# Last three MoE blocks added from on-chip rows by one-hot products, the picked rows read back earlier, overflow rows accumulated into the outputs

## What is computed

```python
def hierarchical_moe(h, w_rg, b_rg, w_re, b_re, w_gate, w_up, w_down):
    ...                       # top-1 of 4 groups, top-2 of the 8 experts in it, gate (tokens x 32)
    for g in range(N_EXPERT_GROUPS):
        sl = slice(g * EXPERTS_PER_GROUP, (g + 1) * EXPERTS_PER_GROUP)
        hid = jax.nn.silu(jnp.einsum('td,edf->tef', t, w_gate[sl])) * jnp.einsum('td,edf->tef', t, w_up[sl])
        hid = hid * gate[:, sl, None].astype(hid.dtype)
        out = out + jnp.einsum('tef,efd->td', hid, w_down[sl])

xp = xp + mp[5] * hierarchical_moe(modulate(xp, norm_ffn_g[l], mp[3], mp[4]), ...)   # gate2 * moe
xs = xs + ms[5] * hierarchical_moe(modulate(xs, norm_ffn_g[l], ms[3], ms[4]), ...)
```

## Time and profile before

| | us |
|---|---|
| median of 3 runs | 822.14 (821.49 to 822.38) |
| the profiled execution, own time | 822.25 |
| its span | 820.5 |
| PE busy | 741.6 (90%) |
| DVE busy | 419.3 (51%) |
| ACT busy | 205.7 (25%) |
| POOL busy | 168.1 (20%) |
| the 16 DMA engines, mean over the span | 224 GB/s |

### The profile page before, as it was taken

The page is one execution under the profiler, slowest core; times in us unless marked ns, Lnnn a source line. Parts: engine busy times, 40 slices in busy tenths (PEclk is TensorE's granted clock), DMA queues, the critical chain, the costliest instruction groups (busy, mean ns, idle before and its releaser), DMA issues.

```text
span 820.5 us, 11125 instructions
## 1 busy us (share of the span) xinstructions
PE 741.6 (90%) x4203; PEld 456.2 (56%) x4203; DVE 419.3 (51%) x928; ACT 205.7 (25%) x417; POOL 168.1 (20%) x192
## 2 busy tenths in 40 slices
PE   4999988999999997999999999886999999999760
PEld 2344455578865655787888344544555555554320
DVE  4123399998799989300224524874333333332226
ACT  4013233314366775102000212222111111111100
POOL 2030012050000000253400002544223323322110
PEclk9899999999999999999999999987999999999995
DMA  8952032442056443343132913077999999999928
GB/s 344 406 174 88 1 102 72 150 171 84 24 205 222 189 169 139 113 142 131 60 103 77 367 75 124 28 261 302 425 424 421 426 423 426 424 424 428 397 98 312
DMA packets 25902, 183.63 MB, mean 224 GB/s; under 512 B 6460, under 2 KB 6884, under 8 KB 14456
## 3 DMA queue, kind: packets, MB, share of 16 engines
q1 hardware_dynamic: 15800, 161.06, 49.0%
q0 software_dynamic: 9456, 19.72, 7.2%
q10 hardware_dynamic: 592, 2.13, 0.7%
HBM read 178.59 MB, written 14.12 MB: 235 GB/s over the span
## 4 chain that ended last, share of the span: by engine, by line
PE 75%; DVE 9%; DMA 7%; ACT 4%; issue 2%; SPq 2%; POOL 0%; DVEq 0%; POOLq 0%; ACTq 0%
PE psum L735 22%; PE psum L1216 12%; PE psum L704 11%; PE psum L1230 6%; DMA arena<-in_experts 5%; PE psum L668 3%; PE psum L1117 2%; PE psum L614 2%; PE psum L1209 2%; ACT arena L1578 2%; DVE arena L2581 1%; DVE arena L2069 1%; PE psum L597 1%; DVE arena L2067 1%; DVE arena L2068 1%
## 5 line engine op out<-in xcount | busy, mean ns | idle before, releaser
L735 PE MATMUL psum<-hT,ring 128*128 128x260 f32 x640 | 143.1, 384 | 3.6 <-DVE sstat L2153 3.6
L735 PEld LDWEIGHTS psum<-hT,ring 128*128 128x128 f32 x640 | 120.7, 190 | 25.5 <-issue 6.3
L1578 ACT ACTIVATE arena<-psum 128x512 f32<-128x512 f32 (+10 forms) x130 | 69.4, 563 | 232.7 <-PE psum L735 74.0
L704 PE MATMUL psum<-ring,hT 128*128 128x512 f32 (+1 forms) x256 | 94.0, 520 | 0.0
L1216 PE MATMUL psum<-ring,arena 128*64 128x256 f32 x608 | 71.5, 389 | 3.2 <-DMA ring<-in_experts 3.2
L704 PEld LDWEIGHTS psum<-ring,hT 128*128 128x128 f32 x256 | 47.6, 191 | 44.9 <-issue 36.0
L1230 PE MATMUL psum<-arena 128*64 128x512 f32 x280 | 67.8, 605 | 3.3 <-issue 2.0
L1517 POOL DMA_INDIRECT expert_rows<-arena,router x35 | 35.3, 1008 | 156.3 <-DVE arena L2541 156.3
L1216 PEld LDWEIGHTS psum<-ring,arena 128*64 128x64 f32 x608 | 44.2, 140 | 34.1 <-issue 9.7
L2540 DVE SCALAR_TENSOR_TENSOR arena<-psum,router,arena 128x512 f32<-128x512 f32 x35 | 26.3, 751 | 64.6 <-PE psum L1230 64.6
L735 PE MATMUL psum<-arena,ring 128*128 128x260 f32 x256 | 58.6, 391 | 0.0
(11 more groups left out here) (380 smaller groups left out, 952.2 us busy)
## 6 DMA issues: line engine op xcount, KB each, us to landing
ring<-in_stream SPq DMA_DIRECT2D x21, 2048.0 KB, 7.9
ring<-in_experts SPq DMA_DIRECT2D x16, 2048.0 KB
arena<-in_experts SPq DMA_DIRECT2D x32, 1024.0 KB
arena<-in_experts SPq DMA_DIRECT2D x11, 2048.0 KB
hT<-in_experts SPq DMA_DIRECT2D x5, 2048.0 KB
ring<-expert_rows SPq DMA_DIRECT2D x8, 512.0 KB, 6.9
ring<-in_stream SPq DMA_DIRECT2D x2, 1280.0 KB, 5.6
arena<-in_x_prompt SPq DMA_DIRECT2D x4, 512.0 KB, 5.8
```

Source lines behind the costliest of these rows:

```text
L704: mm = pe.matmul(psum[:, b, 0:width], hT[:, k, t * P:(t + 1) * P], w[:, k, :], start=(k == 0), stop=(k == KD - 1))
L735: mm = pe.matmul(psum[:, b0 + s, 0:HALF], w[:, k, f * P:(f + 1) * P], rhs[:, k, s * HALF:(s + 1) * HALF], start=(first and k == 0), stop=( ...
L1578: ins = act.activation(out, in_, func, scale=scale)
```

## The change

1. Blocks 32, 33 and 34 (`N_LAST` = 3) are no longer scattered. Their scaled rows stay in three buffers (`y_of`: both `y_rows` and the free down buffer of pipeline place 29). For each of them DVE builds, at steps 6, 7 and 8, five one-hot matrices (`last_hots`: 128 x 128 for each prompt tile, 128 x 8 for the samples) that say which of the 128 half rows belongs to which token. After its last down product PE multiplies them with the kept rows (`last_products`): for tile t and block l two products, one for each half, that use 64 partitions and 512 columns each. For the samples PE first adds the picked rows with four products by an identity of 8 x 8.
2. SP waits for 32 scatters instead of 35 and then issues the same ten loads, the samples' last. Its overflow loop is gone; ACT issues these loads inside its own.
3. DVE adds the picked rows of tiles 0 to 2 partly inside the main loop: `add_picked(0,0)` and `(0,1)` behind y_scaled(32) in step 33, `(1,0)` ahead of y_scaled(33) in step 34, `(1,1)` and `(2,0)` ahead of y_scaled(34) in step 35. Then it adds the rest and PE's sums (`add_last`), and finishes with the samples: a product by gate2 and a sum.
4. Since not every pick is now written, the scratch is zeroed first: DVE clears a constant of 128 x 512, and POOL stores it 17 times (16 of 256 KB) between the second and the third gather of cached keys. gate2 of the samples is stored behind the picks, for the overflow.
5. The overflow pairs, if any, gather the gate with the row and are accumulated straight into the outputs, after these are stored.

```diff
+            def last_products(t, l):
+                n, lead = (P, 2 * t) if t < NT else (NS, 0)
+                pe.wait_ge(y_out, N_MAIN - N_LAST + l + 1)
+                for h in range(2):
+                    rows = slice(SB * h, SB * h + SB)
+                    mm = pe.matmul(psum[0:n, lead + h, :], last_hot[l][t][rows, 0:n], y_of[l][rows, :],
+                                   start=(l == 0 and t < NT), stop=(l == N_LAST - 1))
+                if l == N_LAST - 1:
+                    banks.filled(mm, ("last", t))
+            for t in range(NT - 1):
+                banks.begin(pe, ("last", t), 2 * t, 2 * t + 1)
+                last_products(t, 0)
+                last_products(t, 1)
+            for t in range(NT - 1):
+                last_products(t, 2)
+            banks.begin(pe, ("last", NT - 1), 6, 7)
+            for l in range(N_LAST):
+                last_products(NT - 1, l)
+            banks.begin(pe, ("last", NT), 0, 1)
+            pe.wait_ge(picked_in[NT], 32)
+            for c in range(2):
+                for h in range(2):
+                    pe.matmul(psum[0:NS, h, :], ident[0:NS, 0:NS], picked[c][NT][0:NS, 512 * h:512 * h + 512], ...)
+            for l in range(N_LAST):
+                last_products(NT, l)
 ...
-            over_pairs(sp, sp_pair)
-                sp.wait_ge(y_stored[i], 16 * ((N_MAIN + 1 - i) // 2))
+                sp.wait_ge(y_stored[i], 16 * ((N_MAIN - N_LAST + 1 - i) // 2))
 ...
+                    pool.wait_ge(qi_dup_ready, 2)
+                    for a in range(4 * TOK // P):
+                        store(picks[a * P:a * P + P, :], zeros)
+                    store(picks[4 * TOK // P * P:4 * TOK, :], zeros[0:4 * TOK % P])
 ...
+            pool.wait_ge(outs, 16 * n_outs[0])
+            banks.wait_drained(pool, ("adaS", 10))
+            store(io["expert_rows"][2 * TOK:2 * TOK + NS, :], gate2_s[0:NS])
 ...
-                if b >= 1:
+                if 1 <= b <= N_MAIN - N_LAST:
                     pool.wait_ge(y_out, b)
                     scatter(b - 1)
 ...
+            dve.wait_ge(qi_dup_ready, 1)
+            dve.memset(zeros, 0.0).then_inc(qi_dup_ready, 1)
 ...
+            def last_rows():
+                lane.then(dve.tensor_scalar(last_u, sent[:, LAST_LABEL:LAST_LABEL + N_LAST], C("half_at"), 0.5, ...))
+                for t in range(T5):
+                    lane.mark(dve.tensor_scalar(last_at[:, t], last_u, SKIP / 2 - P * t, None, ALU.add))
 ...
+            def add_picked(t, c):
+                if c == 0:
+                    dve.wait_ge(picked_in[t], 32)
+                lane.wait()
+                lane.mark(dve.tensor_tensor(x2[:, t, :], x2[:, t, :], picked[c][t], ALU.add))
 ...
                     hidden_out(1 - p, hT_out)
+                if b == N_MAIN:
+                    add_picked(1, 1)
+                    add_picked(2, 0)
 ...
                     hidden_of(p, hidden_done)
+                if b == N_MAIN - 1:
+                    add_picked(1, 0)
 ...
                 elif b == 3:
                     over_sent_to()
-            for _, rows, t in LAST_ORDER:
-                ...
+                elif 6 <= b < 6 + N_LAST:
+                    last_hots(b - 6)
+                elif b == N_MAIN - 2:
+                    add_picked(0, 0)
+                    add_picked(0, 1)
+            add_picked(2, 1)
+            add_picked(3, 0)
+            add_last(0)
+            add_picked(3, 1)
+            add_last(1)
+            add_last(2)
+            add_last(3)
+            banks.wait_full(dve, ("last", NT))
+            tmp, x = sample_rows[0:NS], halves(x2[0:NS, NT, :])
+            banks.drained(dve.tensor_tensor(tmp, psum[0:NS, 0:2, :], halves(gate2_s[0:NS]), ALU.mult), ("last", NT))
+            banks.wait_drained(dve, ("last", NT))
+            dve.tensor_tensor(x, x, tmp, ALU.add).then_inc(y_ready, 1)
```

More of the change, by code:

```diff
@@ L93 @@
 SKIP = 8192.0
+N_LAST = 3
 BUFFERS = 6
@@ L119 @@
 assert len(BLOCKS) == N_MAIN
+LAST_LABEL = BLOCKS[-N_LAST][1]
+assert [label for _, label, _, _ in BLOCKS[-N_LAST:]] == [LAST_LABEL + i for i in range(N_LAST)]
 LAST_BLOCK = {p: b for b, (p, _, _, last) in enumerate(BLOCKS) if last}
@@ L1528, in _ @@
                     gather(b + X_BUFFERS)
[L1529 removed]
+                if 1 <= b <= N_MAIN - N_LAST:
                     pool.wait_ge(y_out, b)
                     scatter(b - 1)
[L1532 to L1533 removed]
+            pool.wait_ge(outs, 16 * n_outs[0])
             pool.sem_inc(over_go, 1)
             def pool_pair(i):
[L1537 to L1538 removed]
+                lone_wait(pool, y_outs, 16 * T5, over_passed)
                 for j in range(2):
@@ L1542, in pool_pair @@
                     pool.tensor_copy(next_dest[:, j:j + 1], dest_tab[:, column]).then_inc(over_copied, 1)
-                lone_wait(pool, over_copied, i * 4 + 4, over_passed)
+                    pool.tensor_copy(sample_rows[:, j, :], gate2_h).then_inc(over_copied, 1)
+                lone_wait(pool, over_copied, i * 8 + 6, over_passed)
+                for j in range(2):
+                    pool.tensor_scalar(next_gate[:, j:j + 1], next_dest[:, j:j + 1], 4 * TOK, None, ALU.add)\
+                        .then_inc(over_copied, 1)
+                lone_wait(pool, over_copied, i * 8 + 8, over_passed)
                 for j in range(2):
@@ L2470, in gate_rows @@
                 banks.wait_drained(dve, "gate_items")
-                is_sample(sent, N_MAIN)
+                dve.wait_ge(tables_ready, 1)
+                gate, gate_s = gate_tab[:, 0:N_MAIN], sample_gate[:, 0:N_MAIN]
+                lane.then(dve.tensor_copy(sent, token_tab[:, 0:N_MAIN]))
+                lane.then(dve.scalar_tensor_tensor(gate_s, sent, 2.0 * SEQ, gate, ALU.is_ge, ALU.mult))
+                lane.then(dve.tensor_tensor(gate, gate, gate_s, ALU.subtract))
+                last_rows()
             def over_places():
@@ L2537, in hidden_out, with y_scaled, add_last @@
                 dve.tensor_copy(hidden_T[:, p], psum[:, 4 + p, 0:2 * SB].rearrange("p (f n) -> p f n", f=2)).then_inc(done, 1)
-            def y_scaled(p, gate, gate_s, done):
-                lane.then(dve.scalar_tensor_tensor(y_rows[:, p, :], psum[:, 6 + p, :], gate, gate2_h, ALU.mult, ALU.mult))
-                dve.scalar_tensor_tensor(y_rows[:, p, :], psum[:, 6 + p, :], gate_s, y_rows[:, p, :], ALU.mult, ALU.add)\
-                   .then_inc(done, 1)
+            def y_scaled(y, p, gate, gate_s, done):
+                lane.then(dve.scalar_tensor_tensor(y, psum[:, 6 + p, :], gate, gate2_h, ALU.mult, ALU.mult))
+                dve.scalar_tensor_tensor(y, psum[:, 6 + p, :], gate_s, y, ALU.mult, ALU.add).then_inc(done, 1)
+            def add_picked(t, c):
+                if c == 0:
+                    dve.wait_ge(picked_in[t], 32)
+                lane.wait()
+                lane.mark(dve.tensor_tensor(x2[:, t, :], x2[:, t, :], picked[c][t], ALU.add))
+            def add_last(t):
+                lane.wait()
+                banks.wait_full(dve, ("last", t))
+                x = halves(x2[:, t, :])
+                banks.drained(dve.tensor_tensor(x, x, psum[:, 2 * t:2 * t + 2, :], ALU.add), ("last", t))
             for name in (("adaP", 10), ("adaP", 11), ("adaS", 10)):
```

114 lines of the change are left out of this document (63 added, 51 removed).

## The result

The changed kernel takes 827.36 us (median of 4 runs, 826.38 to 829.79) beside 821.85 for the kernel before on the same chip (median of 4, 821.49 to 822.38): a ratio of 1.0079, 95% interval 1.0046 to 1.0112. By the medians it is 5.5 us slower, by the ratio of the runs taken side by side 0.8%. The forecast was 828.1 with a range of 822.5 to 832.0.

What follows compares the result with a forecast made beforehand. Bound: a closing chain of waits, with PE idle for the last 24.95 us. Span 820.7 (PE's end) + 2.6 + 2.9 + 0.3 = 826.5, 6.0 over 820.5; 822.14 + 6.0 = 828.1 us, range 822.5 to 832.

Steps and rivals of the forecast that it cites:

- The stop: Ahead of down(33): PE stands 6.2 us, since hidden_out(33) is queued behind tile 0's adds, which wait for the picks.
- When the picks land: Tile 0's read-back: lands at 792.8 us, queued behind weights that hold the last engine until 790.
- The lower end of 785.2: Soonest landing of tile 0's picks: scatter 31 landed at 781.2, plus 0.5 and 3.5 us from issue to landing.
- in time, faster: Rival at tile 0's adds: picks land by 786.9, no stall ahead of hidden_out(33), 820.0 us; chance 0.12.
- The clock behind the stop: At down(33) and just after: low clock following PE's stop adds 2.2 us, bounds 0 to 4.2.
- PE's tail: Behind down(34): 15 product pairs 13.5 us, identity products 3.4, hand-overs 0.1; 17.0 us in all, ending at 820.7.
- The end: Behind PE's last product: two DVE instructions with hand-overs 2.6 us, then the 32 KB store and closing 2.9 us.
- the 0.3 from the first blocks: First blocks: `last_rows` puts six small DVE instructions ahead of hidden_out(0), shifting the end by 0.3 us.
- The step on PE's overflow loop: Program end on PE: the loop takes 5.2 us after the last product, ending at 826.2, close behind DVE's end.
- A short stall: Rival ahead of down(33): tile 0 at 791.3, clock stays up, 824.2 us, no change; chance 0.18.
- The serial halves: Rival in PE's last products: the two halves don't run side by side, 13.5 us more, 841.6 us; chance 0.04.
- the zeros: Rival at POOL's 17 early stores: they hold the key gathers 3 to 9 us, 833 us; chance 0.04.

Runs made afterwards that it cites:

- e1: Changed kernel with the five adds of picked rows moved from the main loop to behind y_scaled(34): 821.97 us, ratio 1.0003 to the kernel before.
- e2: e1 with only DVE's wait for both loads of tile 0 put back in step 33, without the adds there: 828.79 us, ratio 1.0080.
- e7: e5 with samples' products and store ahead of tile 3, N_LAST = 2 (block 32 scattered again), only tile 0's adds in step 35: 823.17 us, ratio 1.0037.
- e12: Changed kernel with the samples' four identity products on all 128 rows, not 8; the stop stays: 825.32 us, ratio 1.0048.
- e9: e5 with the samples' four identity products on all 128 rows instead of 8: 818.28 us, ratio 0.9950.
- e5: Changed kernel with the adds of tile 0 and first of tile 1 behind hidden_out(34) in step 35, the others behind the loop: 820.40 us, ratio 0.9986.
- e11: e9 with the samples' products made ahead of tile 3's and the samples stored ahead of tile 3: 816.98 us, ratio 0.9956.
- e4: Changed kernel with the two loads of tile 0 issued on ACT's own queue ahead of silu(34), not by SP: 830.75 us, ratio 1.0121.
- e8: e5 with the samples' identity products written to 128 columns instead of 8, still 8 rows: 819.69 us, ratio 0.9991.

## Why the prediction was right, and where its steps were not

**The stop: right.** Tile 0 was usable 7.45 us after the start of the last gate and up product (789.66 - 782.21); the forecast was 792.8 - 785.43 = 7.4. PE stood for 6.30 us (forecast 6.2). e1 shows that without this wait the kernel is level with the one before, and e2 that the wait alone, put back into e1, brings the whole loss back.

**When the picks land: the number right by two errors that cancel.** The forecast had SP issue the loads at 781.2, 4.2 us before the last gate and up begins, with the 2.27 us of the earlier trace rows for the scatter. In the changed kernel they are issued 0.4 us after it begins (782.60 and 782.21), 4.6 us later than forecast: scatter 31 was issued at 775.74, and SP went on only 6.86 us behind that. SP's waits name the scatter:

```profile
SPq L1405 <- DMA expert_rows<-arena,router: 28.5, 1, 28.5
```

In e7 the same step takes 787.29 - 783.24 = 4.05 us, with fewer weights under way. The 2.27 us of the earlier trace rows are those of the very last scatter, when the engines are idle. That their load makes the difference is likely, but no run tests it alone. Against this, the loads took 7.1 us from issue to use, where the forecast had 792.8 - 781.2 = 11.6, 4.5 too many: it let the weights hold the engines until 790 and put the picks behind them. e7's 6.0 us with the engines nearly free leave about 1.1 us to the weights. So a landing at the right place was partly luck.

The lower end of 785.2 was out of reach for both reasons. It took the 3.5 us of the earlier trace rows, the shortest of ten loads, two of which move 32 KB and not 512 KB. Even with e7's two times it would have been 778.96 + 4.05 + 6.0 = 789.0, so the rival "in time, faster", which needed 786.9, had no room.

**The clock behind the stop: right in kind, its size within the bounds.** The forecast was 2.2 us. In the changed kernel down(33) took 1.6 us more than usual and down(34) nothing; in e12 1.7 and 1.5. The last down product ended 17.6 us after the last gate and up began, where 803.7 - 785.43 = 18.3 were forecast.

**PE's tail: the term that was mis-sized.** 20.1 us instead of 17.0. The twelve pairs of prompt tiles took 10.50 us, 0.875 a pair, so the halves run side by side as said, a little under the lower bound of 0.90. The Trainium skill (page "TensorE: Matmul & The Clock Gate", section "Part 3: Packing small matmuls - row/col tiling") gives 3.07 times for four row tiles. The prediction's estimate of 1.17 us a pair carried this over to two halves, and that is not borne out here. What was too small are the samples' products: 4.42 + 5.16 us instead of 3.4 + 2.7, because the clock falls under them. e12 shows the cause, with e9 beside it: with 128 rows in the identity's products the tail of PE is 16.7 us, within 0.3 of the forecast.

**The end: 1.1 us too long.** 2.46 us for the two DVE instructions and their hand-overs (forecast 2.6), 2.2 from there to the end of the span (forecast 2.9), and nothing to be seen of the 0.3 from the first blocks. The step on PE's overflow loop failed, without a part in the sum: it was said to need 5.2 us behind PE's last product. The branches of the loop and the end of the program on PE in the changed kernel:

```profile
L588 PEldq COMPARE_BRANCH  x8: 86/224/247, 813.0 to 818.5; - x8
L274 PEldq DRAIN  x1: 1328/1328/1328, 818.6 to 818.6; - x1
```

The drain starts at 818.6, before PE's last product has ended (819.9). PE's sequencer steps through the loop while products are still queued: it begins at 811.1, with the load of the pair count, and takes 7.5 us. In the kernel before it begins at 793.6, with the last down product, and what stood out behind that product were the 5.2 us. Where PE's products are shorter it stands out again, by 2.1 us in e12 (823.8 and 821.7), still ahead of the end of the span.

**The sum.** Stop and last blocks -0.7, PE's tail +3.1, the end -1.1: together 1.3 us more than the 6.0 forecast, which is the 7.3 us of the tail. The spans differ by 4.1 us only, since the profiled execution was 3.2 us early ahead of the tail, within the spread of all kernels. That the median, up by 5.5 us, comes so close to the forecast is partly chance.

**The rivals.** "In time" needs a landing that no run shows. "A short stall" has PE stand for about 4 us and the clock stay up. In e2 PE stands for 3.83 us, and the clock does not stay up: down(33) takes 3.63 us. e2 also has the late adds, so it is no clean test of this rival. The serial halves and the zeros fell.

## What to carry to other kernels

Before a wait for a transfer is written into an engine's order, look at what stands behind it: the same adds cost 5 to 7 us ahead of hidden_out(33) (e1, e5) and nothing behind hidden_out(34), one step later. Don't take the time of a scatter on idle engines for one among weight loads: it was 2.3 us and 6.9 us here. Time a transfer by a row of its own size, with all that is issued beside it. And where PE ends a kernel with products of a few rows, give them all the rows, with zeros in the weights, if the clock is seen to fall under them: it cost nothing and took 1.6 and 1.8 us off the tail here (e9, e11).

## What the runs showed of the hardware that was not expected

- The granted clock of TensorE fell from 1.00 to 0.50 with PE busy for 2.00 of 2.00 us, 1.3 to 3.6 us after products of 8 rows began, in seven kernels that had them behind the last block. In four of these (the changed kernel, e4, e5, e8) PE had not paused ahead of them either; in e7 the clock fell as they began, behind a wait of 3.39 us. With 128 rows it stayed at 1.00 to PE's last product (e9, e11, e12); 128 columns changed nothing (e8). The Trainium skill, page "TensorE: Matmul & The Clock Gate", section "What's actually happening", has the clock follow how busy PE has been; here a PE that was never idle lost it. What exactly the chip looks at, these runs don't settle. The kernel before has such a fall too, much earlier: eight records of 8 rows from 76.96 to 77.75, then 0.50 with PE busy for 1.00 of 1.00 us. There short pauses of PE stand ahead of them (0.96 and 0.29 us), and no run separates the two.

```profile
76.96 0.38 PE L769 MATMUL psum<-const,arena 8*128 8x8 f32 x4 [0.29 <-ACT arena L1578]
78.00:79.00 1.00, 1.00 (x6) 0.88 (x8) 0.00 (x0) 0.05 (x1) 0.00 (x0) 0.50 0.00 0
```

- A scatter's way from its issue to the release of SP took 6.9 us while weights were loading (changed kernel), 4.05 in e7 and 2.3 at the end of the kernel before.
- Loads given to a second queue, with six others issued on the first in the same moment, came into use 3 us later than at the head of the first (10.0 and 7.1 us from issue to use).
- PE's sequencer went through the loop at the end of the program, 7.5 us from 811.1, under its queued products: the drain starts at 818.6, the products end at 819.9.
